# Branch projections of the second block as split products in the one weight stream

## The reference, cut to what matters

```python
def _merge(h, outs, gates, w_br, w_merge, b_merge, w_out):
    b, n = h.shape[:2]
    yb = jnp.stack([o * jax.nn.silu(z) for o, z in zip(outs, gates)], axis=2)
    y = jnp.einsum('bnrw,rwd->bnrd', yb, w_br)
    g = jax.nn.sigmoid(h @ w_merge + b_merge).reshape(b, n, N_BRANCH, D_MODEL)
    return jnp.sum(g * y, axis=2) @ w_out
```

## Time and profile before

| | us |
|---|---|
| median of 3 runs | 1517.21 (1517.01 to 1517.27) |
| time of the profiled execution | 1520.71 |
| its span in the trace | 1518.9 |
| PE busy | 1457.1 (96%) |
| DVE, ACT, POOL busy | 773.2, 620.7, 174.9 |
| mean granted clock of PE | 0.977 |

### The profile page before, as it was taken

The page is one execution under the profiler, slowest core; times in us unless marked ns, Lnnn a source line. Parts: engine busy times, 40 slices in busy tenths (PEclk is TensorE's granted clock), DMA queues, the critical chain, the costliest instruction groups (busy, mean ns, idle before and its releaser), DMA issues.

```text
span 1518.9 us, 24394 instructions
## 1 busy us (share of the span) xinstructions
PE 1457.1 (96%) x10290; PEld 1273.3 (84%) x10290; DVE 773.2 (51%) x1183; ACT 620.7 (41%) x1081; POOL 174.9 (12%) x149
## 2 busy tenths in 40 slices
PE   9999999999899899999899998999999879989998
PEld 8989999999655799999788776777777769869998
DVE  6876555447446665555622556232332563564443
ACT  5555444434355544445422434122221343444442
POOL 0010111001200011110013000111111102201110
PEclk9999999999899999999999998999999989999999
DMA  8435655544487355545222220322312213324542
GB/s 308 139 123 173 216 182 180 167 167 167 154 317 255 135 173 188 182 162 177 94 92 74 73 84 1 111 67 100 111 57 83 83 41 124 131 84 139 178 169 98
DMA packets 55821, 211.15 MB, mean 139 GB/s; under 512 B 6048, under 2 KB 9760, under 8 KB 51360
## 3 DMA queue, kind: packets, MB, share of 16 engines
q1 hardware_dynamic: 54976, 206.40, 39.9%
q10 hardware_dynamic: 736, 3.18, 0.6%
HBM read 208.51 MB, written 1.05 MB: 138 GB/s over the span
## 4 chain that ended last, share of the span: by engine, by line
PE 90%; DVE 5%; ACT 2%; issue 1%; POOL 1%; DMA 0%; SPq 0%; POOLq 0%; ACTq 0%; DVEq 0%
PE psum L293 22%; PE psum L295 22%; PE psum L294 22%; PE psum L2126 5%; PE psum L1147 2%; PE psum L1164 2%; PE psum L1297 2%; PE psum L291 2%; PE psum L292 2%; PE psum L290 2%; PE psum L2109 1%; DVE WL L226 1%; PE psum L1453 1%; PE psum L439 1%; PE psum L1151 1%
## 5 line engine op out<-in xcount | busy, mean ns | idle before, releaser
L293 PE MATMUL psum<-XH,WH 128*128 128x256 f32 (+1 forms) x2176 | 700.0, 322 | 18.7 <-DVE WL L226 8.6
L295 PE MATMUL psum<-XH,WL 128*128 128x256 f32 (+1 forms) x2176 | 673.5, 310 | 0.0
L294 PE MATMUL psum<-XL,WH 128*128 128x256 f32 (+1 forms) x2176 | 673.4, 309 | 0.0
L226 DVE TENSOR_TENSOR WL<-stage,WH 128x1024 fp32r<-128x1024 f32 x318 | 388.5, 1263 | 207.9 <-ACT WH L221 207.8
L293 PEld LDWEIGHTS psum<-XH,WH 128*128 128x128 f32 x2176 | 421.4, 194 | 55.8 <-issue 23.5
L294 PEld LDWEIGHTS psum<-XL,WH 128*128 128x128 f32 x2176 | 422.2, 194 | 26.9 <-issue 7.9
L295 PEld LDWEIGHTS psum<-XH,WL 128*128 128x128 f32 x2176 | 421.4, 194 | 20.3
L221 ACT ACTIVATE WH<-stage 128x1024 fp32r<-128x1024 f32 x318 | 319.1, 1051 | 264.4 <-PE psum L295 201.2
L2224 ACT ACTIVATE arena<-psum,par 128x512 f32<-128x512 f32 (+1 forms) x64 | 37.1, 579 | 210.9 <-PE psum L295 210.9
L2184 DVE TENSOR_TENSOR arena<-psum,arena 128x512 f32<-128x512 f32 (+1 forms) x48 | 26.8, 559 | 159.2 <-PE psum L2126 121.8
L2265 POOL TENSOR_TENSOR arena<-arena 128x512 f32<-128x512 f32 (+1 forms) x48 | 48.7, 1014 | 432.7 <-DVE arena L2184 432.7
(11 more groups left out here) (244 smaller groups left out, 1390.9 us busy)
## 6 DMA issues: line engine op xcount, KB each, us to landing
stage<-w SPq DMA_DIRECT2D x132, 512.0 KB, 4.5
stage<-merge SPq DMA_DIRECT2D x64, 512.0 KB, 4.6
ring<-ada SPq DMA_DIRECT2D x24, 1024.0 KB, 4.9
stage<-in SPq DMA_DIRECT2D x44, 512.0 KB, 4.7
stage<-ab_in SPq DMA_DIRECT2D x24, 512.0 KB, 5.1
stage<-nsa_in SPq DMA_DIRECT2D x20, 512.0 KB, 4.8
ring<-br SPq DMA_DIRECT2D x8, 1024.0 KB, 7.8
stage<-out SPq DMA_DIRECT2D x16, 512.0 KB, 4.6
```

What stands on the lines that cost most here:

```text
L226: e.tensor_tensor(lo, raw, hi.bitcast(F32), ALU.subtract).then_inc(s_lo, 1)
L293: e.matmul(dst, wh, xh, start=start, stop=False)
L294: e.matmul(dst, wh, xl, start=False, stop=False)
L295: return e.matmul(dst, wl, xh, start=False, stop=stop)
```

## The change

The branch weights are put into the `merge` chunks. A chunk of this kind holds 16 blocks of 128 x 128; the stream of a layer's merge is, for every c, branch and m, eight gate blocks and then two branch blocks, in all 320 blocks or 20 chunks in place of 16 chunks and 4 ring loads. The branches are split once, high on ACT and low on DVE, each when the first feature that needs it comes up (c = 0), into space of `ring` and `arena`; y becomes two `product` calls (six F32R matmuls). The order of branches is 0, 3, 2, 1. ACT and DVE call `high_next` and `low_next` for the chunks that `merge_chunks` gives for each pair. PE no longer waits at `mixed`; it waits for the split of each branch before its first y. M is split, in both layers, as each of its tiles is finished, into buffers of its own (MH, ML). SG and T2 move to space in the constants, the squares between the layers to M's space. The ring loads of layer 1 that precede (`sp`, `bsp`) wait in SP's queue for layer 0's merge, behind ten `load_next` of layer 1.

```diff
+        with nc.sbuf_tensor("branches", [128, 4096], F32R) as zh, nc.sbuf_tensor("branches_low0", [128, 2048], F32R) as zl0:
+            zh, zl0 = zh[:, :], zl0[:, :]
         ring = sb("ring", NSLOT * SLOT)
...
+        with nc.sbuf_tensor("merged_low", [128, 4096], F32R) as ml, nc.sbuf_tensor("arena_between", [128, 4096], F32):
+            with nc.sbuf_tensor("merged", [128, 4096], F32R) as mh, nc.sbuf_tensor("branches_low1", [128, 2048], F32R) as zl1:
...
-            FLOW += [(f"merge_{l}", r * 4 + c) for c in range(4) for r in range(4)]
+            FLOW += [(f"merge_{l}", c) for c in range(20)]
...
+        MERGED = (0, 3, 2, 1)
+        def merge_chunks(n):
+            return range(-(-20 * n // 16), -(-20 * (n + 1) // 16))
...
 layer_tensor
-            meet(e, f"l{l}.mixed")
+            def block(dst, xh, xl, k, K, name):
+                nonlocal w, n
+                if n % 16 == 0:
+                    w = Chunk(flow, f"merge_{l}", n // 16, 16)
+                t = product(e, dst, w, n % 16, slice(0, 128), xh, xl, k == 0, k == K - 1)
...
+                if n % 16 == 15:
+                    w.done()
+                n += 1
...
-                        for k in range(2):
-                            t = e.matmul(b[:, 0:NT], wb[:, r, k, j * 128:(j + 1) * 128], L.Z[:, r, k, :], start=k == 0,
-                                         stop=k == 1)
+                        if m == 0:
+                            e.wait_ge(*ve.of(f"z{l}.{i}"))
                         for k in range(2):
+                            block(b[:, 0:NT], L.ZH[i][:, k, :], L.ZL[i][:, k, :], k, 2, f"y{l}.{m}.{i}")
...
 layer_vector
+                for i, r in enumerate(MERGED):
+                    if c == 0:
+                        e.wait_ge(*ac.of(f"z{l}.{i}"))
+                        e.tensor_tensor(L.ZL[i], L.Z[:, r], L.ZH[i].bitcast(F32), ALU.subtract).then_inc(*ve.tick(f"z{l}.{i}"))
+                    for _ in merge_chunks(4 * c + i):
+                        low_next(e, flow)
...
-                        if r == 3 and l == 1 and m % 2:
-                            merged_low(e, ve, L, m, CTX)
+                        if i == 3 and m % 2:
+                            merged_low(e, ve, L, m)
-            if l == 0:
-                for k in range(1, 8, 2):
-                    merged_low(e, ve, L, k, slice(0, 512))
...
 layer_scalar
+                    if c == 0:
+                        e.activation(L.ZH[i], L.Z[:, r], ACT.Copy).then_inc(*ac.tick(f"z{l}.{i}"))
+                    for _ in merge_chunks(4 * c + i):
+                        high_next(e, flow)
...
-                        if r == 3 and l == 1:
+                        if i == 3:
                             e.wait_ge(*gp.of(f"u{l}.{n}"))
-                            e.activation(XH[:, m, CTX], L.M[:, m, :], ACT.Copy).then_inc(*ac.tick(f"M{l}.xh{m}"))
+                            e.activation(L.MH[:, m, :], L.M[:, m, :], ACT.Copy).then_inc(*ac.tick(f"M{l}.xh{m}"))
-            if l == 0:
-                e.wait_ge(*pe.of(f"l{l}.merged"))
-                for k in range(8):
-                    e.wait_ge(*gp.of(f"u{l}.{k // 2 * 8 + 6 + k % 2}"))
-                    e.activation(XH[:, k, :], L.M[:, k, :], ACT.Copy).then_inc(*ac.tick(f"M{l}.xh{k}"))
...
 layer_sync
+            if l == 1:
+                e.wait_ge(*pe.of("l0.merged"))
...
-            for c in range(4):
-                ring_load(e, rings, f"br_{l}.{c}", A[f"br_{l}"][c])
-                for r in range(4):
-                    load_next(e, flow)
-            for c in range(4):
+            for c in range(20 + 4):
                 load_next(e, flow)
```

More of the change, by code:

```diff
@@ L301, in features @@
                     x(k)
-                last = product(e, dst, w, k, slice(c, c + 128), XH[:, k, xs], XL[:, k, xs], k == 0, k == 7)
+                last = product(e, dst, w, k, slice(c, c + 128), parts[0][:, k, xs], parts[1][:, k, xs], k == 0, k == 7)
             last.then_inc(*pe.tick(name))
@@ L1768, in __init__ @@
                 self.nsink = MOD[:, 96:100]
[L1769 to L1773, removed]
+                NT = self.NT
+                self.M = view(4096, 8 * NT, **eight)
+                self.MH, self.ML = [v[:, 0:8 * NT].rearrange("p (k n) -> p k n", k=8) for v in (mh, ml)]
+                self.SG, self.T2 = [[d[:, NT * (2 * i + n):NT * (2 * i + n + 1)] for n in range(2)] for i in range(2)]
+                z = [v[:, 0:w * NT].rearrange("p (r a n) -> p r a n", r=w // 2, a=2) for v, w in ((zh, 8), (zl0, 4), (zl1, 4))]
+                self.ZH, self.ZL = [z[0][:, i] for i in range(4)], [z[1 + i // 2][:, i % 2] for i in range(4)]
                 self.units, self.at = [], []
@@ L1789, in build @@
         LAYERS = [Layer(0), Layer(1)]
+        SQM = [view(4096 + 2048 * v, 2048, **eight) for v in range(2)]
         QUERIES, KEYS, VALUES = (0, 3), 1, 4
         OUTER = ((2, 0), (5, 1))
+        MERGED = (0, 3, 2, 1)
+        def merge_chunks(n):
+            return range(-(-20 * n // 16), -(-20 * (n + 1) // 16))
         def keys_tensor(e, flow, L):
@@ L2169, in layer_vector @@
             for c in range(4):
[L2170 to L2178, removed]
+                for i, r in enumerate(MERGED):
+                    if c == 0:
[3 more added lines that the diff above has]
+                        low_next(e, flow)
+                    for m in (2 * c, 2 * c + 1):
+                        s, u, y = L.SG[n % 2], L.T2[n % 2], banks[f"y{l}.{m}.{i}"][:, 0:NT]
+                        e.wait_ge(*ac.of(f"g{l}.{m}.{i}"))
+                        e.wait_ge(*pe.of(f"y{l}.{m}.{i}"))
+                        if i == 0:
+                            e.tensor_tensor(L.M[:, m, :], y, s, ALU.mult).then_inc(*ve.tick(f"y{l}.{m}.{i}"))
                         else:
@@ L2215, in layer_scalar @@
             for c in range(4):
[L2216 to L2220, removed]
+                for i, r in enumerate(MERGED):
+                    if c == 0:
+                        e.activation(L.ZH[i], L.Z[:, r], ACT.Copy).then_inc(*ac.tick(f"z{l}.{i}"))
+                    for _ in merge_chunks(4 * c + i):
+                        high_next(e, flow)
+                    for m in (2 * c, 2 * c + 1):
+                        e.wait_ge(*pe.of(f"g{l}.{m}.{i}"))
                         if n >= 2:
@@ L2258, in layer_gpsimd @@
             for c in range(4):
[L2259 to L2263, removed]
+                for i in range(4):
+                    for m in (2 * c, 2 * c + 1):
+                        if i > 0:
+                            e.wait_ge(*ve.of(f"y{l}.{m}.{i}"))
                             e.wait_ge(*gp.now())
                             e.tensor_tensor(L.M[:, m, :], L.M[:, m, :], L.T2[n % 2], ALU.add).then_inc(*gp.tick(f"u{l}.{n}"))
-                        if r == 3 and l == 1 and m % 2 == 0:
-                            merged_low(e, gp, L, m, CTX)
+                        if i == 3 and m % 2 == 0:
+                            merged_low(e, gp, L, m)
                         n += 1
-            if l == 0:
-                for k in range(0, 8, 2):
-                    merged_low(e, gp, L, k, slice(0, 512))
             gp.mark(f"l{l}.end")
@@ L2548 @@
         br[0], br[1] = br[0][hd], br[1][hd]
-        arr[f"br_{l}"] = np.ascontiguousarray(br.reshape(4, 2, 128, 4, 256).transpose(3, 2, 0, 1, 4)).reshape(
-            4, 128, 2048)
+        gates = I["w_merge_2"][l].reshape(8, 128, 4, 8, 128)
+        br = br.reshape(4, 2, 128, 8, 128)
+        blocks = [b for c in range(4) for r in (0, 3, 2, 1) for m in (2 * c, 2 * c + 1)
+                  for b in [gates[k, :, r, m] for k in range(8)] + [br[r, k, :, m] for k in range(2)]]
+        arr[f"merge_{l}"] = np.ascontiguousarray(np.stack(blocks).reshape(20, 16, 128, 128).transpose(0, 2, 1, 3)).reshape(
+            20, 128, 2048)
         arr[f"fnet_{l}"] = diag(I["w_fnet_2"][l]).reshape(128, 256)
```

48 lines of the change are left out of this document (23 added, 25 removed).

## The result

The changed kernel takes 1501.1 us (median of 4 runs, 1496.11 to 1501.38) against 1517.22 us: a ratio of 0.9886, 95% interval 0.9866 to 0.9907. It is faster, by 16.1 us where 20.2 were forecast. The time lies in the wider range on record (1493.5 to 1503.5) and 1.6 us outside the forecast's own range (1494.5 to 1499.5). Measured again beside the kernel before on two other chips the ratio was 0.9863 (0.9848 to 0.9878) and 0.9865 (0.9849 to 0.9881), which is 20.5 us under 1518.63 and 20.2 us under 1520.33. The profiled execution took 1501.38 us, its span 1499.6, 19.3 us less than the span before.

The account below looks back on a forecast made before the run. PE's instruction stream was taken to bound both merges. Gains of 10.9 + 4.5 + 5.7 + 0.6 - 1.5 = 20.2 us gave 1497.0 us, own range 1494.5 to 1499.5, wider range 1493.5 to 1503.5.

Parts of the forecast that it names:

- y as split products: Both merges: six products replace y's two float32 matmuls, gaining 10.9 us in layer 0 and 4.5 in layer 1.
- rival 6: Products run at the rate of the removed matmuls, 0.214 us each: 1494.2 us; chance 0.03.
- Rival 4: y's six products take as long as the float32 matmuls, so 15.4 us go: 1512.4 us; chance 0.03.
- The end of layer 0's merge: Before w_out: M split tile by tile hides the chain, no wait or half clock; 5.7 us gained.
- Rival 3: w_out's first product still waits, for M or late weights; 4 to 5.7 us not gained, about 1502; chance 0.07.
- The starts: Start of each merge: PE no longer waits for DVE's last attention result; 0.6 us gained for both layers.
- The new wait: Layer 1's merge only: PE waits 1.5 us for the second branch's split, with bounds of 0 and 3.
- Rival 1: The clock falls in layer 1's new wait, giving 1498.7 us; chance 0.10.
- Weights: Merge weight stream: the next chunk's split after a pair's end stays hidden by 1.5 us; no cost.
- rivals 2 and 5: Splits late at pairs calling two chunks, 1505.5 us, chance 0.12; weight stream bounds layer 1, near 1532, chance 0.04.
- The sum: Whole kernel: the terms add to 20.2 us gained, the profiled execution going from 1520.7 to 1500.5 us.
- the same difference gives: Whole kernel: the runs' median stays 3.5 us below the profiled execution, so 1517.2 - 20.2 = 1497.0 us.

Follow-up runs that it names:

- the experiment: Changed kernel with layer 0's M split behind the whole merge again, into XH and XL: 1503.06 us, ratio 0.9893 to the kernel before.
- the shortened kernel: Changed kernel without the low-weight by high-data product in gates and y of both layers' merges: layer 0's merge 150.7 us, layer 1's 92.3.

## Why the prediction was right, point by point

**y as split products.** Right in place and size. The merge's 232.52 became 221.59, 10.93 us less; 10.9 were forecast. This holds one thing that cancelled: y's own products take 0.233 us and the gates' 0.2275, where the forecast had 0.2287 for all. The merge itself was to take 219.5 us and took 221.59: 32 periods leave out the ten products at its start that ran at the half clock, as some ten did in the kernel before; the second profile, without them, has 219.44. In layer 1 the merge lost 3.34 us; without the new wait (branches split one ahead) it lost 4.99, where 4.5 were forecast, since the new products start every 0.117 us there and not every 0.1196. The faster rate of rival 6 did not come; nor did the Trainium skill's 216 ns (the formula of "TensorE: Matmul & The Clock Gate", Back-to-back issue gap): the six products of y are further from it than g's. Rival 4 is out by the period.

**The end of layer 0's merge.** The mechanism was right: no wait, no half clock, the chain hidden with 1.2 us to spare. The term was mis-sized: 5.69 forecast, 4.48 measured, 4.44 by the experiment; against the second profile of the kernel before it is 5.53. The missing 1.2 us are w_out's own step, 0.2333 us from the new buffers against (1227.64 - 1186.11) / 183 = 0.2269 before, over 191 steps; the forecast had put a change of this step at nothing. Rival 3 is out.

**The starts.** 0.49 us in each layer, by the distance from the last attention matmuls to the first gate product (1.55 and 1.06 us in layer 0, 1.52 and 1.03 in layer 1). The forecast took 0.6 for both and 0.43 in each at most, from the row of idle; that row is a little under what the wait cost.

**The new wait.** Forecast at 1.45 us, by its chain and in layer 1 only; measured 1.37, and in layer 0 none (the second branch is ready at 966.11, PE wants it at 967.27). The parts came as priced, but the copy took 0.63, not 0.53, and the low 0.69, not 0.59. Rival 1 is out: the granted clock of layer 1's merge is 1.00. So an idle of 1.37 us cost 1.6 us and no half clock, where 3.91 us at the seam brought the half clock for eight products and in another execution for 13. (The section "What's actually happening" that rival 1 names is one of the Trainium skill's "TensorE: Matmul & The Clock Gate".) The third branch came 0.7 us ahead of PE. What the Trainium skill ("SBUF — State Buffer", SBUF: two separate sides) has on two inputs against GpSimd went the other way round than feared: DVE's low of the third branch (start 1372.59, 0.68 us) had the start and POOL's two adds beside it took 2.15 us in place of 1.5, which agrees with the page; PE did not wait for them.

**Weights.** No wait for a low of weights in either merge; rivals 2 and 5 are out. The weak place was named rightly, ACT's wait for M at the end of a pair, with 1.5 us to spare forecast and 1.6 measured, and the shortened kernel fails just there.

**The sum.** Against its own execution 19.3 us were measured where 20.2 were forecast. By parts these are 10.9 + 5.0 + 4.5 + 1.0 - 1.65 = 19.7, and 0.55 from the end of layer 1 (29.01 against 28.46 us). The stretches ahead of the two merges gave back 1.0 us; no run traces that, but the same stretches differ by as much between two profiles of the changed kernel. So it was in part luck that the sum of the parts came out so near: the seam was 1.2 too high, layer 1's period and the starts 0.9 too low.

The step behind the sum did not hold, "the same difference gives": the 3.5 us between the profiled execution before and the median of three runs were taken as a property of the kernel. They were a draw of the clock within a spread of 5 us, and did not come again with the changed kernel. Over the other chips the difference of the medians is 20.5 and 20.2 us, though each of these medians can move by a few us. A time of 1501.1 us alone would have fitted rival 3 (about 1502) too; that the forecast's mechanism holds is known from the traces.

The change also reorders the branches and moves SG, T2 and the squares to other places. No run tests these by themselves; none of them shows as a wait of PE.

## What to carry to other kernels

When PE's instruction stream bounds a stage without a gap, count its steps from start to start, and the gain of a cheaper sequence can be told closely (here 10.9 of 10.93 us in one layer, 4.5 of 4.99 in the other). After splitting work into tiles, look at the first place where a queue waits on the bound engine: all that stands behind that wait (here a chunk's split, a table load, two sigmoids) is paid in line, and moving one small operation ahead of it gave 1.6 us back. To learn how much room a stream has, shorten the engine that bounds it, and look where the first waits stand as well as how long the stage takes. Before a difference of a few us is read out of three runs, look how far executions of one and the same kernel lie apart.

## What was not expected of the hardware

- The granted clock differs between executions of the same program at the same place: the first ten products of a merge at 0.43 us or at 0.23 us each, 5 us over the whole kernel between the fastest and the slowest execution. Behind one and the same wait of 3.91 us, 8 products ran at the half clock in one execution and 13 in another.
- The step of an F32R product depends on where its data lie: 0.227 us from XH and XL, 0.233 us from the new buffers at 512 columns; at 256 columns 0.1195 and 0.117, the other way round. Moving the tiles by 4 or 32 bytes each changed the mean by up to 1% at 512 columns and 2% at 256. What in the place or the layout does it is left open.
- DVE's low of a weight half took 1.52 us on average in layer 0's merge before and 1.22 in the changed kernel. Before, 11 of the 16 pairs of lows there began while POOL's add ran, and two lows then took 3.19 us in place of 2.36. In the new order none of them meets an add; two of POOL's adds began behind a low of a branch and took 2.2 us in place of 1.3 (mean 1.37 against 1.29). It was off PE's path both times.
